# Hybrid encoder step: 128-token spans in the gated linear attention, and four smaller edits around the attention and the start

## The reference, cut to what matters

```
def gla_chunk(S, xs):                       # chunks of C = 64 tokens, scanned in order
    qc, kc, vc, gc = xs
    b = jnp.cumsum(gc, axis=2)              # gc: log of the gate, per key channel
    q_e = qc * jnp.exp(b)
    k_e = kc * jnp.exp(-b)
    a = jnp.where(causal, jnp.einsum('bhtd,bhsd->bhts', q_e, k_e), 0.0)
    o = jnp.einsum('bhts,bhsv->bhtv', a, vc) + jnp.einsum('bhtd,bhdv->bhtv', q_e, S)
    b_last = b[:, :, -1:, :]
    S_new = jnp.exp(b_last[:, :, 0, :])[..., None] * S + jnp.einsum(
        'bhsd,bhsv->bhdv', kc * jnp.exp(b_last - b), vc)
    return S_new, o

def attend(q, k, v, bias, valid):
    s = jnp.einsum('bqhd,bkhd->bhqk', q, k).astype(jnp.float32) * ATT_DH ** -0.5 + bias
    s = jnp.where(valid, s, NEG_INF)
    p = jax.nn.softmax(s, axis=-1).astype(v.dtype)
    return jnp.einsum('bhqk,bkhd->bqhd', p, v)
```

## Time and profile before

| | |
|---|---|
| median of three runs | 2697.03 us (2696.6 to 2699.65) |
| profiled execution, device time | 2699.24 us |
| its span, first to last instruction | 2697.5 us |
| PE busy | 2676.2 us, 99% |
| DVE, ACT, POOL busy | 47%, 35%, 6% |
| granted TensorE clock, mean | 0.997 |
| chain that ended last | PE 96%, DVE 3%, ACT 1% |

### The profile page before, as it was taken

One profiled execution on the slowest core, in us unless ns is written; L12 is line 12 of the kernel. 1 busy time (PEld: TensorE's weight loads), 2 busy tenths in 40 slices (PEclk: granted clock), 3 DMA queues, 4 the chain that ended last, 5 costly groups with the idle time before them and its releaser, 6 DMA issues.

```text
span 2697.5 us, 50440 instructions
## 1 busy us (share of the span) xinstructions
PE 2676.2 (99%) x21037; PEld 2591.9 (96%) x21037; DVE 1264.6 (47%) x1717; ACT 955.4 (35%) x1438; POOL 167.8 (6%) x182
## 2 busy tenths in 40 slices
PE   8999999999999999999999999999999999999998
PEld 8999999999888899999999899999999999999998
DVE  5555443344554554334447554433445555442442
ACT  5444321222454432222246542222224544221233
POOL 2101000001000010000022210000011101000001
PEclk9999999999999999999999999999999999999999
DMA  3222233232333222322322222332332223232232
GB/s 112 67 65 79 86 89 91 86 91 84 111 103 98 82 78 86 102 78 86 94 69 74 77 83 78 86 95 83 89 86 74 67 65 91 85 94 82 86 98 77
DMA packets 440461, 229.71 MB, mean 85 GB/s; under 512 B 15780, under 2 KB 436864, under 8 KB 440336
## 3 DMA queue, kind: packets, MB, share of 16 engines
q1 hardware_dynamic: 438688, 226.89, 29.1%
q10 hardware_dynamic: 1200, 0.59, 0.1%
q0 software_dynamic: 448, 0.45, 0.1%
HBM read 219.03 MB, written 8.87 MB: 84 GB/s over the span
## 4 chain that ended last, share of the span: by engine, by line
PE 96%; DVE 3%; ACT 1%; issue 1%; DMA 0%; ACTq 0%; DVEq 0%
PE slot L1794 86%; PE aux L1762 2%; PE aux L1939 1%; PE aux L2021 1%; PE aux L2163 1%; PE aux L1958 1%; PE aux L2169 1%; PE aux L2075 1%; DVE w_lo L1141 1%; PE aux L1954 1%; DVE xg_lo L1153 0%; PE slot L1802 0%; DMA raw<-in_l_gla_w_gate_a_dram 0%; PE aux L1904 0%; PE aux L1829 0%
## 5 line engine op out<-in xcount | busy, mean ns | idle before, releaser
L1794 PE MATMUL slot<-xg_hi,w_hi 128*128 128x272 f32 x4352 | 918.9, 292 | 3.9 <-DVE gla_sq L1159 2.2
L1794 PE MATMUL slot<-xg_hi,w_lo 128*128 128x272 f32 x4352 | 901.0, 289 | 0.0
L1794 PE MATMUL slot<-xg_lo,w_hi 128*128 128x272 f32 x4352 | 898.8, 288 | 0.0
L1794 PEld LDWEIGHTS slot<-xg_hi,w_hi 128*128 128x128 f32 x4352 | 682.6, 189 | 27.2 <-issue 22.1
L1794 PEld LDWEIGHTS slot<-xg_lo,w_hi 128*128 128x128 f32 x4352 | 685.2, 189 | 0.0
L1794 PEld LDWEIGHTS slot<-xg_hi,w_lo 128*128 128x128 f32 x4352 | 680.9, 189 | 0.0
L1141 DVE TENSOR_TENSOR w_lo<-raw,w_hi 128x1024 fp32r<-128x1024 f32 (+3 forms) x368 | 479.4, 1303 | 239.9 <-ACT w_hi L612 231.6
L612 ACT ACTIVATE w_hi<-raw 128x1024 fp32r<-128x1024 f32 (+4 forms) x369 | 409.2, 1109 | 348.9 <-PE slot L1794 334.1
L1794 PE MATMUL slot<-h_hi,w_hi 128*128 128x272 f32 x1386 | 286.2, 288 | 0.0
L1794 PE MATMUL slot<-h_hi,w_lo 128*128 128x272 f32 x1386 | 285.9, 287 | 0.0
L1794 PE MATMUL slot<-h_lo,w_hi 128*128 128x272 f32 x1386 | 285.9, 287 | 0.0
(11 more groups left out here) (303 smaller groups left out, 2359.0 us busy)
## 6 DMA issues: line engine op xcount, KB each, us to landing
raw<-in_l_ffn_w_in_dram SPq DMA_DIRECT2D x176, 512.0 KB, 3.8
raw<-in_l_ffn_w_out_dram SPq DMA_DIRECT2D x64, 704.0 KB, 4.5
raw<-in_l_gla_w_in_dram SPq DMA_DIRECT2D x48, 512.0 KB, 3.7
raw<-in_l_att_w_qkv_dram SPq DMA_DIRECT2D x24, 512.0 KB, 3.7
raw<-in_l_lru_w_in_dram SPq DMA_DIRECT2D x24, 512.0 KB, 3.8
raw<-in_l_gla_w_out_dram SPq DMA_DIRECT2D x16, 512.0 KB, 3.6
raw<-in_l_lru_w_out_dram SPq DMA_DIRECT2D x7, 768.0 KB, 4.7
att_bias<-bias_scratch SPq DMA_DIRECT2D x8, 512.0 KB, 4.0
```

Source lines behind the costliest of these rows:

```text
L1794: ins = pe.matmul(slot[par][:, hf, 0:HALF], w[par][:, k, :], a[:, k0 + k, hf * HALF:(hf + 1) * HALF], start=(k == 0 and at == 0), stop=(k ...
```

## The change

1. Gated layers: the spans of the recurrence are 128 tokens (`NCHUNK = SEQ // P`, 4 in place of 8). `b` still starts anew every 64 tokens, and for the first half of each span DVE subtracts the value at its middle, so that exponents are taken relative to the span's middle. `b_mid` and `b_end` are new small tiles. The corner of `tri` is no longer cleared. `outer` has 128 tokens at a time and `out` one state matmul of 128 columns per tile.
2. Attention: prompt scores of t = 1, 2, 3 are made from q and k split into fp32r parts: ACT makes `q_hi`, `k_hi` (`high_part`), DVE `q_lo`, `k_lo` (`low_part`), and PE three products per head.
3. Attention's output: the `w_lo` of the first full part after the last pair goes to POOL, and later splits stand one place earlier in ACT's and DVE's order.
4. Start: ACT squares rows 2 and 3 after the third and fourth part of x; DVE copies the first part of x before it splits the gate's weights.

The diff, cut to its core:

```diff
-NCHUNK = SEQ // CHUNK
+NCHUNK = SEQ // P
...
+        QK_COLS = (("q", slice(DEC_SEQ, TOK)), ("k", slice(0, SEQ)))
-        OUTER_BANK = (A1, A2, A3, A0, A1, A2, A3, A2, A0)
+        OUTER_BANK = (A1, A2, A3, A1, A0)
@@ scalar, start @@
+            for t in (QT, 0, 1):
+                row_square(t)
+            split(0, 0, "low")
...
             x_part(2)
+            row_square(2)
             x_part(3)
             x_copy(5)
             x_part(4)
+            row_square(3)
@@ scalar, decays @@
-                    act.wait_ge(s_b, q + 1)
+                    act.wait_ge(s_bm, q + 1)
@@ scalar, attention @@
+                def high_part(j, n):
+                    name, cols = QK_COLS[n]
+                    act.wait_ge(s_free, b0 + 3 * j + n + 1)
+                    if j:
+                        act.wait_ge(s_sm, (j - 1) * 2 * ITEMS + 2 * QT)
+                    act.activation(AT[name + "_hi"][:, :], AT[name][j % 2][:, cols], ACT.Copy).then_inc(s_qkh, 1)
...
+                        if n in (15, 19):
+                            high_part(j, (15, 19).index(n))
...
                 for m in range(EARLY, XT):
-                    if m > EARLY:
-                        split_out(i, b0, m + 2)
+                    if m < XT - 1:
+                        split_out(i, b0, m + 3)
@@ vector, start @@
+            x_copy(0)
             split(0, 0, "low")
-            x_copy(0)
@@ vector, cumsum @@
-                    dve.tensor_tensor(GL["z"][:, 0:SEQ].rearrange("p (c n) -> p c n", n=CHUNK),
-                                      GL["b"][:, CHUNK - 1:SEQ:CHUNK].unsqueeze(2).broadcast_to([P, NCHUNK, CHUNK]),
-                                      GL["b"][:, 0:SEQ].rearrange("p (c n) -> p c n", n=CHUNK), ALU.subtract)
+                    spans = GL["b"][:, 0:SEQ].rearrange("p (c n) -> p c n", n=P)
+                    dve.tensor_copy(b_mid[:, :], GL["b"][:, CHUNK - 1:SEQ:P])
+                    dve.tensor_copy(b_end[:, NCHUNK - 1:NCHUNK], GL["b"][:, SEQ - 1:SEQ])
+                    dve.tensor_tensor(b_end[:, 0:NCHUNK - 1], GL["b"][:, P - 1:SEQ - P:P], GL["b"][:, P + CHUNK - 1:SEQ:P],
+                                      ALU.add).then_inc(s_mid, 1)
+                    dve.wait_ge(s_mid, q + 1)
+                    dve.tensor_tensor(spans[:, :, 0:CHUNK], spans[:, :, 0:CHUNK],
+                                      b_mid[:, :].unsqueeze(2).broadcast_to([P, NCHUNK, CHUNK]), ALU.subtract).then_inc(s_bm, 1)
+                    dve.wait_ge(s_bm, q + 1)
+                    dve.tensor_tensor(GL["z"][:, 0:SEQ].rearrange("p (c n) -> p c n", n=P),
+                                      b_end[:, :].unsqueeze(2).broadcast_to([P, NCHUNK, P]), spans, ALU.subtract)
@@ vector, attention @@
+                def low_part(j, n):
+                    name, cols = QK_COLS[n]
+                    dve.wait_ge(s_qkh, 2 * j + n + 1)
+                    dve.tensor_tensor(AT[name + "_lo"][:, :], AT[name][j % 2][:, cols], AT[name + "_hi"][:, :].bitcast(F32),
+                                      ALU.subtract).then_inc(s_qkl, 1)
...
+                        if n in (18, 22):
+                            low_part(j, (18, 22).index(n))
...
-                split_out(i, b0, EARLY + 1)
...
+                dve.wait_ge(s_lo, out + EARLY + 2)
                 split_out(i, b0, EARLY + 2)
@@ tensor, outer and out @@
-                    rows = slice(c % 2 * CHUNK, c % 2 * CHUNK + (CHUNK if c < NCHUNK else DEC_SEQ))
+                    rows = slice(0, P if c < NCHUNK else DEC_SEQ)
...
-                    if 3 <= c < NCHUNK:
-                        pe.wait_ge(s_s, q * (NCHUNK + 1) + (c - 2 if c < 7 else 7))
+                    if c == 3:
+                        pe.wait_ge(s_s, q * (NCHUNK + 1) + 2)
...
-                    for c in (2 * t, 2 * t + 1):
-                        if c:
-                            cols = slice(c * CHUNK, (c + 1) * CHUNK)
-                            ins = pe.matmul(bank[:, cols], GL["s"][:, c - 1, vj], qe[:, cols], start=False, stop=bool(c % 2))
+                    if t:
+                        cols = slice(t * P, (t + 1) * P)
+                        ins = pe.matmul(bank[:, cols], GL["s"][:, t - 1, vj], qe[:, cols], start=False, stop=True)
@@ tensor, attention scores @@
+                    if t == 1:
+                        pe.wait_ge(s_qkl, 2 * j + 2)
+                    if 0 < t < QT:
+                        at, keys = slice(SEQ - (t + 1) * P, SEQ - t * P), slice(0, (t + 1) * P)
+                        for n, (qn, kn) in enumerate((("q_hi", "k_hi"), ("q_lo", "k_hi"), ("q_hi", "k_lo"))):
+                            for e in range(2):
+                                rows = slice(64 * e, 64 * e + 64)
+                                if n == 0:
+                                    pe.wait_ge(s_sc, 2 * z - 1 + e)
+                                ins = pe.matmul(SCORE_BANK[e][:, keys], AT[qn][rows, at], AT[kn][rows, keys],
+                                                start=(n == 0), stop=(n == 2))
@@ gpsimd, attention @@
+                b = b0 + 3 * PAIRS + EARLY + 1
+                pool.wait_ge(s_hi, b + 1)
+                pool.wait_ge(s_lo, b)
+                pool.tensor_tensor(w_lo[b % 2][:, 0:XT, :], raw[b % 2][:, 0:XT, :], w_hi[b % 2][:, 0:XT, :].bitcast(F32),
+                                   ALU.subtract).then_inc(s_lo, 1)
```

More of the change, by code:

```diff
@@ L637, in _, with row_square @@
             act.wait_ge(s_cd, 1)
-            for n, t in enumerate((QT, *range(QT))):
-                if t == 2:
-                    split(0, 0, "low")
+            def row_square(t):
                 rows = SAMPLE if t == QT else ALL
@@ L713, in decays @@
                     act.activation(GL["enb"][:, :], GL["b"][:, :], ACT.Exp, scale=-1.0 / GATE_TAU)
-                    act.activation(dec[:, 0:NCHUNK], GL["b"][:, CHUNK - 1:SEQ:CHUNK], ACT.Exp, scale=1.0 / GATE_TAU)
+                    act.activation(dec[:, 0:NCHUNK], b_end[:, :], ACT.Exp, scale=1.0 / GATE_TAU)
                     act.activation(dec[:, NCHUNK:], GL["b"][:, TOK - 1:TOK], ACT.Exp, scale=1.0 / GATE_TAU).then_inc(s_e, 1)
@@ L878, in attention @@
                 split(b0 + 3, (b0 + 1) % 2, XT)
+                high_part(0, 0)
+                high_part(0, 1)
                 decay_abs()
@@ L1372, in head_step @@
                         state(h, NCHUNK)
-                    if n in (47, 49, 51, 53):
-                        state(h, n - 47)
-                        state(h, n - 46)
+                    if n == 47:
+                        state(h, 0)
+                        state(h, 1)
+                    if n in (49, 51):
+                        state(h, (n - 45) // 2)
                     if n == 69:
@@ L1936, in outer @@
                             pe.wait_ge(s_z, q + 2)
-                    if 3 <= c < NCHUNK:
-                        pe.wait_ge(s_s, q * (NCHUNK + 1) + (c - 2 if c < 7 else 7))
-                    pe.matmul(OUTER_BANK[c][:, 0:GLA_DV], GL["kd_t"][rows, c // 2, :], GL["v_t"][rows, c // 2, :],
+                    if c == 3:
+                        pe.wait_ge(s_s, q * (NCHUNK + 1) + 2)
+                    pe.matmul(OUTER_BANK[c][:, 0:GLA_DV], GL["kd_t"][rows, c, :], GL["v_t"][rows, c, :],
                               start=True, stop=True).then_inc(s_um, 1)
@@ L1953, in out @@
                             pe.matmul(A2[:, cols], s_in[:, vn], qe[:, SEQ:TOK], start=False, stop=True)
[L1954 to L1958 removed]
+                    ins = pe.matmul(bank[:, t * P:(t + 1) * P], GL["v_t"][:, t, vj], GL["at"][:, t, :], start=True, stop=(t == 0))
+                    if t:
+                        cols = slice(t * P, (t + 1) * P)
+                        ins = pe.matmul(bank[:, cols], GL["s"][:, t - 1, vj], qe[:, cols], start=False, stop=True)
                     if t == QT - 1:
@@ L1981, in head_step @@
                         outer(h, NCHUNK)
-                    if n in (46, 48, 50, 53):
-                        c = 2 * (46, 48, 50, 53).index(n)
-                        outer(h, c)
-                        outer(h, c + 1)
+                        outer(h, 0)
+                        outer(h, 1)
+                    if n == 48:
+                        outer(h, 2)
+                        outer(h, 3)
                     if n in (55, 57, 59, 61):
@@ L2019, in scores @@
                             pe.wait_ge(s_sc, 2 * z - 1 + e)
-                        if t < QT:
-                            ins = pe.matmul(bank[:, 0:(t + 1) * P], q[rows, TOK - (t + 1) * P:TOK - t * P], k[rows, 0:(t + 1) * P],
-                                            start=True, stop=True)
-                        else:
-                            pe.matmul(bank[SAMPLE, 0:PAST], q[rows, 0:DEC_SEQ], AT["kc_t"][rows, :], start=True, stop=True)
-                            ins = pe.matmul(bank[SAMPLE, PAST:PAST + DEC_SEQ], q[rows, 0:DEC_SEQ], k[rows, SEQ:TOK],
-                                            start=True, stop=True)
-                        ins.then_inc(s_sm, 1)
```

(6 more changed lines are left out.)

20 lines of the change are left out of this document (14 added, 6 removed).

## The result

| | before | after |
|---|---|---|
| device time, median of 4 runs (us) | 2697.95 | 2665.82 |
| lowest and highest | 2696.60, 2699.65 | 2664.84, 2666.61 |
| profiled execution: span, device time | 2697.5, 2699.24 | 2663.1, 2664.84 |

What follows compares the result with a forecast made beforehand. The prediction took PE, busy 2676.2 of 2697.5 us, as the bound. Savings of 22.1 + 3.8 + 3.0 + 1.6 = 30.5 us from 2697.0 gave 2666.5 us, range 2661 to 2678.

Steps and rivals of the forecast that it cites:

- gated layers: Outer products and `out` insertions of the gated heads: 2.76 us saved a head, 22.1 us for eight heads.
- scores: Attention's prompt scores: three fp32r passes replace four float32 passes, 0.48 us saved a pair, 3.8 us for eight pairs.
- attention's output: After the last pair: moving splits removes PE waits of 1.27 and 1.46 us; 3.0 us saved, bounds 1.3 and 3.2.
- start: Kernel start: `xg_hi` no longer waits for two squares on ACT; 1.6 us saved, bounds 0 and 2.1.
- `outer` term: Gated heads' outer products: fewer half-height switches at 0.30 us, a head from 3.54 to 2.44, saving 1.10 us.
- `out` term: Gated heads' `out` insertions: 22 float32 matmuls become 14, eight at 0.208 us, saving 1.66 us a head.
- half of the gated part: Rival in gated layers: 128-column state matmuls cost more, `out` saves 1.0 a head, kernel 2672 us; chance 0.10.
- The head's cover: Gated heads: of 4.4 us between `kd` ready and PE turning it, 2.8 stay, so DVE's added work costs nothing.
- None of the 0.29 growing: Score groups: the 0.29 us each float32 group has beyond its stream stays the same with three fp32r passes.
- rival that second and third rounds wait 0.104 for their weights: Score groups: weight waits add 0.6 to 0.9 us a pair, kernel 2671.5 to 2674; scores without gain had chance 0.20.
- The first low step is before 13.2 us: Sign of being right at the kernel's start: PE's first low step before 13.2 us, forecast at about 12.9.

Runs made afterwards that it cites:

- e2_scores: Kernel before with only the attention's rounding and three-pass fp32r prompt scores changed; 2694.57 us, ratio 0.9985.
- e3_out: Kernel before with only the attention's output changed, a split moved to POOL; 2696.31 us, ratio 0.9991.
- e7_sample_grouped: Changed kernel with the sample's four output matmuls of a head ordered by height, second value tile in another bank; 2666.12 us, ratio 0.9881.
- e1_gated: Kernel before with only the gated layers' 128-token spans; 2675.12 us, ratio 0.9913.
- e5_no_start: Changed kernel with the start as it was before; 2668.08 us, ratio 0.9891.
- e4_start: Kernel before with only the start's order of first squares and copies changed; 2697.47 us, ratio 0.9994.
- e6_heads_in_turn: Changed kernel with all passes of one head ahead of the other's in each three-pass score group; 2667.47 us, ratio 0.989.

## Why the prediction was right, and where it was off

The steps in the order of its sum, by the pieces that repeat:

| term | forecast | measured | from |
|---|---|---|---|
| gated layers | 22.1 | 25.2 | heads, 12.6 in each of two layers |
| scores | 3.8 | 3.0 alone, 2.8 in the full change | e2_scores; pair 29.27 to 28.91 |
| attention's output | 3.0 | 2.8 | e3_out |
| start | 1.6 | 1.0 on average, standard error 0.8 | fourteen openings |
| stream | 0 | -1.1 | below |
| sum | 30.5 | 30.7 | |

The three profiles of each kernel differ by more, 2697.4 - 2665.3 = 32.1 us in the mean of the spans, as do the medians: the changed kernel's three openings were 2.4 us shorter than the other's, of which the fourteen give the edit 1.0 and the rest is the clock's.

**Gated layers: right in its mechanism, two unit prices low.** The `outer` term was mis-sized, 1.10 for 1.40 a head. By the reading to the second pair the insertions cost 1.45 + 3 x 0.83 = 3.94 before and 1.68 + 0.86 = 2.54 after. The prediction read each of the four before to the first pair behind it, which is drawn about 0.1 us early. To the second pair a pair of 64-row products costs 0.83 - 0.427 = 0.40 beyond its stream, not 0.30, and the changed kernel's first insertion has that once: 1.68 - 3 x 0.427 = 0.40, while the second has none, 0.86 - 2 x 0.427. Four insertions too low by 0.1 before and one after hid 0.3 us of the gain, which is the whole difference. The `out` term was 1.66 for 1.79: four insertions of 6.34 in all became 4.55, which for eight matmuls is 0.224 each, not 0.208. The sum, 3.19, agrees with the 3.15 of the heads.

The Trainium skill, "TensorEngine Tiling (Array Packing)", Theoretical Speedup, against which the prediction set the price of the trace, would have made this term nothing: two side by side for one of full height is an even trade of streams. Yet the joining gained 1.40 a head, and e7_sample_grouped got 0.24 from one change of height and back without touching any stream. Its Key Properties, on the drain when the mode changes, fit that too. Why the price is 0.40 around two 64-row products and 0.24 in the sample's step was not tested.

The rival named as half of the gated part was priced at 2672 us, a loss of 5.5 of the 22.1, so its name and its price do not agree; the measured `out` term, 1.79 a head rather than 1.0, rules out both.

**The head's cover held.** No wait of PE follows `kd`; what DVE gained in work cost nothing. The same head as in the earlier trace rows, in the changed kernel's timelines of POOL and PE:

```profile
114.79 1.35 POOL L2400 TENSOR_TENSOR gla_kd<-gla_k,gla_ekd 128x544 f32<-128x544 f32 x1
...
119.61 0.63 PE L1806 MATMUL aux<-ident,gla_kd 128*128 128x128 f32 x4
```

`kd` is ready at 116.14 and turned at 119.61: of 4.4 us of cover 3.5 are left, where the prediction expected 2.8.

**Scores: right, mis-sized by a fifth to a quarter.** One pass is saved as forecast, but each group has about 0.04 us more on top than the float32 group had: by the same reading t = 1 went from 0.82 to 0.74, a saving of 0.08 for a pass of 0.107. "None of the 0.29 growing" was the step that was off (read to the second pair, that 0.29 is 0.39 in the float32 group of t = 1 and 0.42 in the fp32r one). The rival that second and third rounds wait 0.104 for their weights did not come. The rule that stood beside it, that a load overlaps a running matmul only where the row group differs (the Trainium skill, "TensorE: Matmul & The Clock Gate", Part 3), would have given that loss; the groups don't show it.

**Attention's output: right.** Both waits are gone, with 0.9 us between the end of POOL's split and PE's need of it.

**Start: right on the wait (1.4 us of the 1.6), but it was not the whole opening.** The first low step is before 13.2 us, as the prediction asked, in only three of the seven profiles with the edit, and at 13.49 in the mean, not at 12.9. What the prediction did not see is that the granted clock there changes from execution to execution. With the edit's own share that makes the 4.8 us of the first profile, and it accounts for most of the distance between its span, 2663.1, and the forecast one, 2667.0; the two other profiles of the same program have 2667.5 and 2665.3, the mean of the three being 2665.3. So that 2665.8 came so close to 2666.5 is partly luck, by errors that cancel: gated 3.1 more, the other three terms 1.6 to 1.8 less, the stream 1.1 back.

**The stream: a loss that no term had.** With the gated edit, unbroken pieces of k-steps far from any edited line became longer. In the chain, before and then in the changed kernel:

```profile
1577.74 58.53 PE slot L1794 x468
```

```profile
1555.22 59.00 PE slot L1838 x468
```

The same 468 matmuls take 0.47 us more; a piece of 210 takes 0.18 more, the two of 3144 and the one of 3108 take 0.1 more each, the one of 2694 0.08. Kernels with the gated edit have it (e1_gated 59.01, e5_no_start 59.01), those without don't (e2_scores and e3_out 58.55, e4_start 58.53). The clock is 1.00 in both, and no row shows a wait. In all it is 17.1 - 12.6 - 2.8 - 2.8 = -1.1 us, nearly all of it in these pieces. Its cause was not tested and stays open.

## What to carry to other kernels

Where PE is the bound, count small matmuls there as two things: the matmuls themselves, which on all rows cost 0.22 us each in float32 up to 128 columns, and each change from full-height to part-height tiles and back, 0.24 to 0.4 us in this kernel. Group the part-height ones, and let full-height ones stand where they suit the other engines. Read the price of an insertion to the second matmul pair behind it, and compare kernels by pieces of the chain that repeat from execution to execution; the opening, where the clock moves by itself, needs many executions: seven profiles of a kind did not tell 1.0 us from nothing.

## What the runs showed of the hardware that was not expected

- Matmuls on one half of the rows do not wait for those on the other half that stand ahead of them in the program: in e6_heads_in_turn both heads' first pass starts at 722.9 us.
- The granted clock in the first 36 us differs between executions of one program: 1.00, 0.79 and 0.59 in the stretch from 13.0 to 21.2 us for the changed kernel, and the opening with it, by up to 4.4 us.
- Merging two insertions of full-height matmuls gains nothing (0.1 us over eight heads), where grouping the part-height ones of a head gains 0.24 us a head.
- Long streams of the same matmuls can be 0.03% to 0.8% longer in one program than in another, at the same clock and without a wait.
